# Hybrid attention and recurrence step on one core: recurrence outputs and half of its keys turned by VectorE blocks and scratch memory instead of TensorE

## The reference, cut to what matters

```python
def step(S, inp):                      # chunks of the sequence; h: 4 heads of 128 keys x 128 values
    qc, gc, kc, vc = inp
    L = jnp.cumsum(gc, axis=1)
    o_inter = jnp.einsum('bchk,bhkv->bchv', qc * jnp.exp(L), S)
    ...                                # A: decayed scores inside the chunk
    o_intra = jnp.einsum('bhij,bjhv->bihv', A, vc)
    Lc = L[:, -1]
    S_new = jnp.exp(Lc)[..., None] * S + jnp.einsum('bjhk,bjhv->bhkv', kc * jnp.exp(Lc[:, None] - L), vc)
    return S_new, o_inter + o_intra

yb = rms_norm(o, o_norm_g).reshape(B, T, WIDTH_B) * jax.nn.silu(zb)
g_a, g_b = jnp.split(jax.nn.sigmoid(h @ w_merge + b_merge), 2, axis=-1)
y = g_a * (ya @ w_proj_a) + g_b * (yb @ w_proj_b)
out = x + gate * (y @ w_out)
```

## Time and profile before

| what | value |
|---|---|
| median of 3 runs (lowest, highest) | 1558.33 us (1558.32, 1558.43) |
| span of the profiled execution | 1555.9 us |
| PE busy | 1527.1 us, 98% of the span |
| DVE, ACT, POOL busy | 51%, 35%, 53% |
| DMA | 178.94 MB, 33% of the 16 engines' time |

### The profile page before, as it was taken

One profiled execution on the slowest core, in us unless ns is written; L12 is line 12 of the kernel. 1 busy time (PEld: TensorE's weight loads), 2 busy tenths in 40 slices (PEclk: granted clock), 3 DMA queues, 4 the chain that ended last, 5 costly groups with the idle time before them and its releaser, 6 DMA issues.

```text
span 1555.9 us, 31655 instructions
## 1 busy us (share of the span) xinstructions
PE 1527.1 (98%) x13048; PEld 1243.0 (80%) x13048; DVE 787.0 (51%) x1900; ACT 540.7 (35%) x1119; POOL 826.0 (53%) x1074
## 2 busy tenths in 40 slices
PE   5999999999999999999999999999999999999998
PEld 2777788877888788888779878888888978888886
DVE  4767464234558866232544774622453775623132
ACT  4334324334322532434331452243432353143330
POOL 0525434557863643365773472437786363437671
PEclk9999999999999999999999999999999999999999
DMA  9612211334453321233343231223544231222351
GB/s 339 243 55 83 83 57 55 111 133 158 168 197 108 110 70 57 82 109 108 137 164 135 92 120 43 83 66 114 208 154 149 75 110 56 78 72 91 102 167 60
DMA packets 62790, 178.94 MB, mean 115 GB/s; under 512 B 7086, under 2 KB 18695, under 8 KB 61864
## 3 DMA queue, kind: packets, MB, share of 16 engines
q1 hardware_dynamic: 62648, 176.93, 33.4%
HBM read 162.84 MB, written 11.96 MB: 112 GB/s over the span
## 4 chain that ended last, share of the span: by engine, by line
PE 95%; DVE 3%; DMA 1%; SPq 1%; issue 1%; ACT 0%; DVEq 0%
PE ps_D L758 56%; PE ps_D L755 25%; PE ps_XCD L820 2%; PE ps_XB L896 1%; PE ps_XB L949 1%; PE ps_XA L954 1%; PE ps_XA L921 1%; PE ps_XA L932 1%; PE ps_XB L948 1%; PE ps_XA L896 1%; DMA th_t<-in_w_ada 1%; SPq L507 1%; PE ps_XB L932 0%; PE ps_XCD L831 0%; PE ps_XCD L939 0%
## 5 line engine op out<-in xcount | busy, mean ns | idle before, releaser
L1702 POOL TENSOR_TENSOR w_lo_t<-w_raw,w_hi_t 128x256 fp32r<-128x256 f32 x920 | 681.0, 775 | 599.7 <-ACT w_hi_t L980 599.4
L758 PE MATMUL ps_D<-h_hi_t,w_hi_t 128*128 128x512 f32 x1024 | 411.2, 402 | 0.0
L758 PE MATMUL ps_D<-h_hi_t,w_lo_t 128*128 128x512 f32 x1024 | 399.6, 390 | 0.0
L758 PE MATMUL ps_D<-h_lo_t,w_hi_t 128*128 128x512 f32 x1024 | 399.5, 390 | 0.0
L980 ACT ACTIVATE w_hi_t<-w_raw 128x1024 fp32r<-128x1024 f32 x232 | 240.0, 1051 | 124.6 <-PE ps_D L755 61.6
L758 PEld LDWEIGHTS ps_D<-h_hi_t,w_hi_t 128*128 128x128 f32 x1024 | 192.3, 188 | 46.3 <-issue 8.9
L758 PEld LDWEIGHTS ps_D<-h_hi_t,w_lo_t 128*128 128x128 f32 x1024 | 192.2, 188 | 41.8
L758 PEld LDWEIGHTS ps_D<-h_lo_t,w_hi_t 128*128 128x128 f32 x1024 | 192.6, 188 | 36.5
L755 PE MATMUL ps_D<-w_hi_t,h_hi_t 128*128 128x384 f32 (+1 forms) x384 | 141.6, 369 | 1.0 <-DVE yf_t L1342 1.0
L755 PE MATMUL ps_D<-w_lo_t,h_hi_t 128*128 128x384 f32 (+1 forms) x384 | 136.6, 356 | 0.0
L755 PE MATMUL ps_D<-w_hi_t,h_lo_t 128*128 128x384 f32 (+1 forms) x384 | 136.3, 355 | 0.0
(11 more groups left out here) (386 smaller groups left out, 2332.9 us busy)
## 6 DMA issues: line engine op xcount, KB each, us to landing
w_raw<-in_w_blocks SPq DMA_DIRECT2D x232, 512.0 KB, 3.4
xr<-in_x_prompt SPq DMA_DIRECT2D x16, 512.0 KB, 5.0
x_or_AT<-in_x_prompt SPq DMA_DIRECT2D x14, 512.0 KB, 4.8
out_dram<-xr SPq DMA_DIRECT2D x12, 512.0 KB, 2.8
x_or_AT<-in_x_turned SPq DMA_DIRECT2D x3, 1024.0 KB, 5.6
p_or_hf<-in_x_turned SPq DMA_DIRECT2D x3, 1024.0 KB, 6.2
out_dram<-xr SPq DMA_DIRECT2D x8, 256.0 KB, 2.0
ibtok<-vtok SPq DMA_DIRECT2D x8, 192.0 KB, 3.5
```

The lines of the kernel that those rows point to most:

```text
L758: ins = mm(bank[:, :], w[:, s0, k0 + k, :], a[:, k, :], start=go, stop=end)
L1702: ins = g_.tensor_tensor(w_lo[:, c, k:k + 2], w_raw[:, n % NRAW, k:k + 2], f32(w_hi[:, c, k:k + 2]), ALU.subtract)
```

## The change

Two of the four `KT` tasks (t = 2, 3) and all four `yT` go from TensorE. In their place:

- VectorE transposes blocks of 32x32 in place in `kk`, 128x1024 elements in one instruction: once for the keys of tiles 2 and 3 (`kD`), and once for each half of the outputs at the end of `onorm`, which is now two tasks of two tiles.
- The 32x32 blocks still have to trade places. ScalarE's queue writes the half to scratch memory in HBM (`ks`, `os`: one transfer of 512 KB), and reads it back when that has landed (`kl`, `ol`: four transfers of 128 KB, each to 32 partitions, in runs of 32 floats, which is 128 bytes, so 1024 runs each). The keys go to `k_turned`, the outputs of the first half to the space of `acc` and `kst`, those of the second to that of `qq`.
- VectorE then multiplies with the gate out of SBUF (`yD`), and ScalarE and GpSimd make the two parts (still called `yT`) at the half units 66, 67, 70 and 71, where they stood at 67, 68, 69 and 70.

```diff
+KEYS_TURNED = (1,)
+O_AT, ON_AT, YD_AT, YT_AT = (57, 59, 61, 63), (60, 64), (65, 66, 69, 70), (66, 67, 70, 71)
+KS_AT, KL_AT, OS_AT, OL_AT = (56, 56), (57, 57), (61, 65), (63, 67)
...
     for _t in range(NT):
-        put(it, 28 + _t, 0, "KT", _t, "XC")
-        put(it, 28 + _t, 1, "o", _t, "XB")
-        put(it, 28 + _t, 1, "st", _t, "XA")
-    put(it, 32, 0, "onorm", 0)
+        if _t // 2 not in KEYS_TURNED:
+            put(it, 28 + _t, 0, "KT", _t, "XC")
+        at_half(it, O_AT[_t], "o", _t, "XB")
+        at_half(it, O_AT[_t], "st", _t, "XA")
+    for _r in KEYS_TURNED:
+        at_half(it, 56, "kD", _r)
+    for _r in range(2):
+        at_half(it, ON_AT[_r], "onorm", _r)
+        if _r in KEYS_TURNED:
+            at_half(it, KS_AT[_r], "ks", _r)
+            at_half(it, KL_AT[_r], "kl", _r)
+        at_half(it, OS_AT[_r], "os", _r)
+        at_half(it, OL_AT[_r], "ol", _r)
     for _t in range(NT):
-        at_half(it, 67 + _t, "yT", _t, "XB" if _t % 2 else "XA")
+        at_half(it, YD_AT[_t], "yD", _t)
+        at_half(it, YT_AT[_t], "yT", _t)
...
+    zk, zo = (nc.dram_tensor(f"z_{n}", [2, 4, 32, 2 * HB, 4, 32], F32).ap() for n in "ko")
...                                          # TensorE
                 elif task == "st":
-                    s.freed(it, "KT", a)
+                    if a < 2:
+                        s.freed(it, "KT", a)
+                    else:
+                        s.wait_ge("kt_in1", 64 * (it + 1))
                     for h in range(HB):
-                        ins = mm(bank[:, P * h:P * h + P], kst[:, h, :], ibtok[:, a, P * h:P * h + P],
+                        left = kst[:, h, :] if a < 2 else k_turned[:, 1, h, a % 2, :]
+                        ins = mm(bank[:, P * h:P * h + P], left, ibtok[:, a, P * h:P * h + P],
                                  start=True, stop=True)
-                elif task == "yT":
-                    s.wait_ge("on", 4 * it + a + 1)
-                    for h in range(HB):
-                        ins = tr(bank[:, P * h:P * h + P], kk[:, h, P * a:P * a + P], ident[:, :])
...                                          # ScalarE
+                elif task == "ks":
+                    s.wait_ge("kD", len(KEYS_TURNED) * it + KEYS_TURNED.index(a) + 1)
+                    s.wait_ge(f"kt_in{a}", 64 * it)
+                    load(zk[a].rearrange("i q (h t) j p -> (i q) h (t j p)", t=2), kk[:, :, 256 * a:256 * a + 256], f"kz{a}")
+                elif task == "kl":
+                    s.wait_ge(f"kz{a}", 16 * (it + 1))
+                    for j in range(4):
+                        load(k_turned[32 * j:32 * j + 32, a].rearrange("p h t (i c) -> p (h t) i c", c=32),
+                             zk[a, :, :, :, j].rearrange("i q n p -> q n i p"), f"kt_in{a}")
+                elif task == "os":
+                    s.wait_ge("oD", 2 * it + a + 1)
...                                          # the same store and load for the outputs
                     for h in range(HB):
-                        ins = fn(acc[:, P * h:P * h + P], bank[:, P * h:P * h + P], ACT.Square,
+                        ins = fn(yf[:, 1, P * h:P * h + P], bank[:, P * h:P * h + P], ACT.Square,
                                  accum_out=oss[:, HB * a + h:HB * a + h + 1])
...                                          # VectorE
+                elif task == "kD":
+                    half = kk[:, :, 256 * a:256 * a + 256]
+                    do(v.transpose(half, half), "kD")
                 elif task == "onorm":
-                    s.freed(it, "o", 3)
...
+                    s.freed(it, "o", 2 * a + 1)
+                    c, half = slice(8 * a, 8 * a + 8), kk[:, :, 256 * a:256 * a + 256]
...
+                    do(v.transpose(half, half), "oD")
-                elif task == "yT":
-                    s.full(*key)
-                    free(stt(yf_slot(16 * it + 4 + a), bank[:, 0:512].rearrange("p (h n) -> p h n", h=HB), og_half[:, 0:1],
-                             szb[:, :, P * a:P * a + P], ALU.mult, ALU.mult), *key)
+                elif task == "yD":
+                    s.wait_ge(f"ot_in{a // 2}", 64 * (it + 1))
+                    do(stt(yf_slot(16 * it + 4 + a), o_turned[a // 2][:, :, a % 2], og_half[:, 0:1],
+                           szb[:, :, P * a:P * a + P], ALU.mult, ALU.mult), "yt")
```

More of the change, by code:

```diff
@@ L379, in build @@
         qa, q3 = (yf[:, :, c:c + w].rearrange("p s (n d) -> p s n d", d=DH) for c, w in ((0, 384), (384, 128)))
-        acc = sb("acc_t", [P, TB])
-        kst = sb("kst_t", [P, HB, P])
+        acc_kst = sb("acc_or_kst", [P, 2 * TB])
+        acc, kst = acc_kst[:, 0:TB], acc_kst[:, TB:].rearrange("p (h n) -> p h n", h=HB)
         hS, yS = sb("hS_or_yS", [P, KT, 32]), sb("cT_or_ab", [P, KT, 32])
@@ L392, in build @@
         ps_s = kst[0:8]
-        AT32 = kst[:, :, :].rearrange("p h (t i) -> p (h t) i", t=NT)
+        AT32 = kst.rearrange("p h (t i) -> p (h t) i", t=NT)
         sq_in = ibS[:, 0:256]
@@ L406, in build @@
         first.close()
+        k_turned = first.enter_context(nc.sbuf_tensor("k_turned", [P, 2, HB, 2, P], F32))
+        first.close()
+        first = ExitStack()
         yb_hi, yb_lo = sb("yb_hi_t", [P, 4, TB], F32R), sb("yb_lo_t", [P, 4, TB], F32R)
@@ L414, in build @@
         szb = qT
+        o_turned = [t.rearrange("p (h t n) -> p h t n", h=HB, t=2)
+                    for t in (acc_kst[:, :], qq.rearrange("p h n -> p (h n)")[:, 0:1024])]
+        zk, zo = (nc.dram_tensor(f"z_{n}", [2, 4, 32, 2 * HB, 4, 32], F32).ap() for n in "ko")
         y_hi, y_lo = sb("y_hi_t", [P, KT, TB], F32R), sb("y_lo_t", [P, KT, TB], F32R)
@@ L1001, in h_high_half, with load @@
                 s.done(fn(h_hi[:, k, P * t:P * t + P], hf[t % 2][:, k], ACT.Copy), "h_hi")
+            def load(dst, src, name):
+                s.done(act.dma_start(dst, src), name, by=16)
             s.wait_ge("x_in0", 16)
@@ L1109, in side @@
                     s.done(fn(ses, ses, ACT.Exp), "s_exp")
+                elif task == "ks":
[9 more added lines that the diff above has]
+                    s.wait_ge("oD", 2 * it + a + 1)
+                    s.wait_ge(f"ot_in{a}", 64 * it)
+                    load(zo[a].rearrange("i q (h t) j p -> (i q) h (t j p)", t=2), kk[:, :, 256 * a:256 * a + 256], f"oz{a}")
+                elif task == "ol":
+                    s.wait_ge(f"oz{a}", 16 * (it + 1))
+                    s.full(it, "o" if a else "st", 3 if a else 1)
+                    for j in range(4):
+                        load(o_turned[a][32 * j:32 * j + 32].rearrange("p h t (i c) -> p (h t) i c", c=32),
+                             zo[a, :, :, :, j].rearrange("i q n p -> q n i p"), f"ot_in{a}")
                 elif task == "qtA":
@@ L1126, in side @@
                     s.full(*key)
-                    if it or a:
-                        s.full(*((it, "st", a - 1) if a else (it - 1, "st", 3)))
-                    s.free(fn(kst[:, :, :], bank[:, :].rearrange("p (h n) -> p h n", h=HB), ACT.Copy), *key)
+                    if a:
+                        s.full(it, "st", a - 1)
+                    s.free(fn(kst, bank[:, :].rearrange("p (h n) -> p h n", h=HB), ACT.Copy), *key)
                 elif task == "o":
@@ L1169, in _ @@
                             if task == "yT":
-                                s.freed(it, "yT", a)
+                                s.full(it, "st", 3)
+                                s.wait_ge("yt", 4 * it + a + 1)
                                 high(yb_hi[:, :, P * a:P * a + P], 16 * it + 4 + a)
@@ L1547, in side @@
                     free(ins, *key)
+                elif task == "kD":
+                    half = kk[:, :, 256 * a:256 * a + 256]
+                    do(v.transpose(half, half), "kD")
                 elif task == "onorm":
-                    s.freed(it, "o", 3)
-                    do(ts(oss, oss, 1.0 / P, EPS, ALU.mult, ALU.add))
-                    rsqrt(orst, oss, ow1, ow2)
-                    for t in range(NT):
-                        o = kk[:, :, P * t:P * t + P]
-                        s.done(tt(o, o, orst[:, HB * t:HB * t + HB].unsqueeze(2).broadcast_to([P, HB, P]), ALU.mult), "on")
-                elif task == "yT":
-                    s.full(*key)
-                    free(stt(yf_slot(16 * it + 4 + a), bank[:, 0:512].rearrange("p (h n) -> p h n", h=HB), og_half[:, 0:1],
-                             szb[:, :, P * a:P * a + P], ALU.mult, ALU.mult), *key)
+                    s.freed(it, "o", 2 * a + 1)
+                    c, half = slice(8 * a, 8 * a + 8), kk[:, :, 256 * a:256 * a + 256]
+                    do(ts(oss[:, c], oss[:, c], 1.0 / P, EPS, ALU.mult, ALU.add))
+                    rsqrt(orst[:, c], oss[:, c], ow1[:, c], ow2[:, c])
+                    for t in (2 * a, 2 * a + 1):
+                        o = kk[:, :, P * t:P * t + P]
+                        s.done(tt(o, o, orst[:, HB * t:HB * t + HB].unsqueeze(2).broadcast_to([P, HB, P]), ALU.mult))
+                    s.settle()
```

(2 more changed lines are left out.)

5 lines of the change are left out of this document (4 added, 1 removed).

## The result

The kernel before takes 1558.3 us and the changed one 1569.0 us, both on the same chip; the ratio is 1.0067, with a 95% interval from 1.0053 to 1.0081. The forecast was 1559.6 us, with a range up to 1568.0. So the changed kernel is slower by 10.7 us where no measurable change was forecast, and it lies just outside the range. Its four executions took 1565.7, 1569.0, 1569.0 and 1569.6 us; the profile is of one of 1569.0.

What follows compares the result with a forecast made beforehand. The prediction took TensorE's list to bound the kernel: 1558.3 us, less 10.8 us of transposes, plus 12.0 us of new stall, gave 1559.5, forecast as 1559.6 us (+0.1%), with a range from 1555.0 to 1568.0 us.

Steps and rivals of the forecast that it cites:

- What bounds the kernel: Whole kernel: the chain of waits runs over TensorE for 95% of the span, with no hidden slack.
- The gain: TensorE's list: 24 groups of four transposes go, at 0.45 us each, 10.8 us off.
- The stall: At `pb0`: TensorE waits for the last `yb_lo`, behind GpSimd's split of `pa2`; 12.0 us added over four iterations.
- The clock: Behind the stall at `pb0`: granted clock falls to half, 2 to 3 us each time, total 1564 to 1566; chance 0.10.
- The second outputs' load: Issued behind unit 33: takes about 6 us against 8.0 us of room, so it is hidden.
- rival 1: Second outputs' load lands late, from run price or queueing behind weights; stall 4.1 to 5.4 us, total 1562.7 to 1567.9; chance 0.21.
- The price of a run of 128 B: In the scratch-memory loads: 15 ns a run, between next to nothing and 26 ns.
- The rule that I drew from it: For the loads: a 128 B run costs no less than a 512 B run (26 ns), so the second load is late.
- The costs taken as nothing: VectorE's block transposes (1.35 us each), ScalarE's 15 issues per iteration, the stores and the keys' load: 0 us.
- rival 3: At `pb0`: the stall is absent or small; total 1547.5, or up to 1555 with half of it; chance 0.14.

Runs made afterwards that it cites:

- the best version: Changed kernel with the last `yT` at 70 instead of 71 and the next `x` tiles' loads at unit 37 instead of 33: 1548.9 us, ratio 0.9937.
- `x` later alone: Changed kernel with only the loads of the next `x` tiles issued four units later (37 instead of 33), last `yT` still late: 1565.7 us, ratio 1.0052.
- before, `yT` late: Kernel before the change, with its last `yT` at half unit 71 instead of 70: 1572.5 us, ratio 1.0092.
- `FILL = 4`: Changed kernel with 4 extra matmuls (0.9 us) on TensorE ahead of the wait for `yb_lo` at `pb0`: 1564.0 us, ratio 1.0031.

## Why the prediction was wrong

- **What bounds the kernel: right.** TensorE's list did; both its removed work and its new waits appear one for one.
- **The gain, 24 x 0.45 = 10.8 us: right as a sum, partly by luck.** In the third and fourth iteration units 30 to 35 are 2.97 us shorter, so a group was worth 0.50 us. The first gave only 2.1 us, since `o` 1 now waits 1.3 us for ScalarE, a wait that I had at zero. All four gave 10.8 us, and the best version (1548.9) is 9.7 us below before. Part of the gain is lost elsewhere: TensorE has two waits of its own instruction queue in the second iteration that came with the changed list (last section).
- **The stall, 3 x 3.3 + 2.1 = 12.0 us: right in place, cause and nearly in size.** It was 3.35, 2.17, 4.52 and 3.55 us, 13.6 together. The chain over unit 35, the split of `pa2` and the last `yb_lo` was read from the order and priced from the earlier trace rows, and moving one entry of the order took it away, with the transfers in place.
- **The clock: this is the step that failed.** The forecast took the half clock as a rival with a chance of 0.10, because "dense matmuls stand right ahead and behind", and its sum has no term for it. The runs show 8.7 us for it, in three of four stalls. The rows were there: a wait of 2.6 us and then 0.50 for 6.8 us. The argument against it had no row behind it. Its price of 2 to 3 us each was right (2.7 to 2.9), and with three of four stalls in it the forecast would have been 1559.5 + 8.7 = 1568.2. One reading in the rival was loose: the wait does not lie ahead of the fall of the clock. It lasts from 37.55 to 40.16, and the clock falls at 38.6, in its midst, as it does in the stalls of the changed kernel:

```profile
40.16 1.97 PE L709 MATMUL ps_XA<-ident,s_st_lo 128*128 128x128 f32 x8 [2.61 <-DVE p_or_hf L1253]
```

- **The second outputs' load: the room was right, the time too short.** I took 6 us against 8.0 us of room. It takes 6.1 us in the first and 7.9 us in the fourth iteration, with weights alone beside it, and 10.1 and 10.2 us in the two between, beside `x`. Two things were missing. The fourth transfer is issued only 2.8 to 3.4 us behind the first, a cost that I had put on ScalarE but not on the load. And the `x` beside it, above. So the late half of rival 1 came true by one of its two causes, other loads on the engines (`x` rather than weights), and not by the price of a run. Of the lateness only 1.2 us reached TensorE in the third iteration and 0.2 us in the fourth; in the second other work covers it.
- **The price of a run of 128 B: near the guess.** I took 15 ns, from between nothing and 26 ns. From 249 to 252 us the keys' load is alone on the engines; 2660 runs took 71.2% of them (packets, MB, share of 16 engines), so a run took 0.712 x 16 x 3.0 us / 2660 = 12.9 ns:

```profile
q10 hardware_dynamic: 2660, 0.34, 71.2%
```

The Trainium skill ("DMA: Bandwidth & Descriptors", Specifications) says that below 512 B the DMA engines read, modify and write. The rule that I drew from it, that a small run costs no less than one of 512 B, does not hold here: it costs half as much. But it carries a quarter of the bytes, so per byte it is twice as dear.
- **The costs taken as nothing: right.** A block transpose of 1024 columns took 1.25 us (1.35 expected), and the keys' load was never waited for. Three of ScalarE's issues took up to 6.8 us together (first outputs, first iteration), and ScalarE emptied the bank of unit 32 behind them, 1.4 us later than it else does, but no unit of TensorE grew by it.
- **A small slip in rival 3.** With half of the stall its total is 1547.5 + 6.0 = 1553.5 us, not 1555.

## What to carry to other kernels

When a step goes from TensorE's list, write down for every hand-over behind it which instruction it now queues behind on the helping engines; here one entry of the order was worth 17.6 us, more than the change itself. Add up a set of transfers as the issues ahead of the last one plus its own landing. Price a new stall of TensorE twice, once as the gap and once as the half clock behind it, and give the second no small chance when a row of the same trace shows it. Look at what else is queued on the DMA engines in the stretch where a transfer has little room.

## What the runs showed of the hardware

- **The clock behind a stall.** TensorE was dense ahead of and behind every stall. Idle times at `pb0`, and how long the granted clock was 0.50 around the end of them:

| idle us | kernel | half clock |
|---|---|---|
| 4.4, 3.4, 3.2 | changed | 6.8 us each |
| 3.4, 3.2, 3.2 | `x` later alone | half as long; 6.8 us; 6.8 us |
| 2.7, 2.7, 2.7 | before, `yT` late | half as long; none; none |
| 2.9, 2.2, 2.2 | `FILL = 4` | half as long; half as long; none |
| 2.0 or less | all of them | none |

The length of the gap alone does not decide: 2.2 and 2.7 us went with half as long or none, 3.4 us with 6.8 us or half as long. Nor does the fall start at a fixed place: 0.8 to 1.2 us ahead of the end of the stall in the changed kernel, 1.0 us behind it in the kernel before with `yT` late. This would also make executions of one kernel differ by 1 to 3 us, as they did.
- **Issues on ScalarE's queue.** The first transfer of 1024 runs takes 0.59 us to issue, the next 0.70 us, and the later ones up to 3.7 us while the engines are full. At those times ScalarE's next instruction waits behind them: it sat idle for 4.3 us in the third iteration of the changed kernel and for 6.1 us in the first (of the latter, 1.4 us were a real delay, as unit 32 ended at 282.89 only). In these rows "issue" means that the profile shows no other engine that it waited for.

```profile
1056.78 0.63 ACT L1092 ACTIVATE yb_hi_t<-yf_t 128x512 fp32r<-128x512 f32 x1 [4.28 <-issue]
...
284.44 0.69 ACT L1070 ACTIVATE th_t<-ps_D,bm_half 128x512 f32<-128x512 f32 x1 [6.09 <-issue]
```

- **Waits of TensorE's instruction queue.** Gaps of 0.5 to 1.6 us stand in or right behind runs of small matmuls (32 or 16 columns), where TensorE waits for nothing that the profile shows. They depend on the list as well as on the execution. Two of them, in units 19 and 23 of the second iteration, stand in all eight traces of kernels with the changed list (these units take 9.2 to 9.9 and 7.6 to 8.1 us) and in neither of the two with the list of before (8.0 and 8.6, 6.9 and 6.9 us). They are there without any transfer too (9.3 and 8.0 us), so the transfers don't make them; what does is open. The changed kernel's two gaps:

```profile
576.05 0.32 PE L898 MATMUL ps_XCD<-qq,kk 128*32 128x32 f32 x11 [1.60 <-issue]
603.63 0.30 PE L916 MATMUL ps_XB<-qq,kk 128*32 128x16 f32 x12 [0.67 <-issue]
```

Others differ in size from trace to trace. Two kernels that differ by less than 2 us can't be told apart by one trace each.
